# Delta rule: the meta tokens' inverse moved out of the two-by-two level sequence, lower weight halves of the next head held back in the scan, small copies and exponentials moved between engines

## The reference, cut to what matters

```python
qkv = silu(depthwise_conv(concat([q, k, v]), conv_w))     # 5 taps
q, k = l2norm(q) * DN_DK ** -0.5, l2norm(k)
b = cumsum(g)                                            # per chunk
dec = where(incl, exp(b_i - b_j), 0)
A = where(strict, (k * beta) @ k.T * dec, 0)
sol = triangular_solve(A + I, rhs)                       # the inverse
attn = (q @ k.T) * dec
def step(S, inp):                                        # over chunks
    v_new = uc - wc @ S
    o = qd @ S + attn @ v_new
    S = S * cd + kd.T @ v_new
```

## Time and profile before

| | us |
|---|---|
| median of 3 runs | 2447.34 |
| lowest and highest of them | 2438.19, 2450.72 |
| the profiled execution's own time | 2440.41 |
| its span | 2438.6 |

### The profile page before, as it was taken

The page is one execution under the profiler, slowest core; times in us unless marked ns, Lnnn a source line. Parts: engine busy times, 40 slices in busy tenths (PEclk is TensorE's granted clock), DMA queues, the critical chain, the costliest instruction groups (busy, mean ns, idle before and its releaser), DMA issues. The chain is left out here.

```text
span 2438.6 us, 43070 instructions
## 1 busy us (share of the span) xinstructions
PE 2276.5 (93%) x14129; PEld 1347.7 (55%) x14129; DVE 1612.6 (66%) x3480; ACT 1011.7 (41%) x1779; POOL 1037.3 (43%) x732
## 2 busy tenths in 40 slices
PE   7999998996888888888999999998999999999998
PEld 6444444455767777774465556555666544444443
DVE  7535333115666666661522798898999589999887
ACT  4322323314343434423313433437899544443331
POOL 4421421414444445434613687776676422222220
PEclk9999999998999999999999999999999999999999
DMA  5311311311110111004331698888999799999994
GB/s 200 120 53 51 103 55 55 104 51 34 35 35 26 34 34 34 9 1 139 121 113 45 191 316 283 283 291 266 385 395 353 241 368 383 385 388 388 344 358 151
DMA packets 174313, 440.38 MB, mean 181 GB/s; under 512 B 17408, under 2 KB 83584, under 8 KB 174096
## 3 DMA queue, kind: packets, MB, share of 16 engines
q1 hardware_dynamic: 132752, 288.20, 34.5%
q0 software_dynamic: 36864, 134.23, 15.3%
q10 hardware_dynamic: 4608, 16.78, 1.7%
HBM read 395.11 MB, written 44.04 MB: 180 GB/s over the span
## 5 line engine op out<-in xcount | busy, mean ns | idle before, releaser
L2193 POOL TENSOR_TENSOR hid_u_lo<-hid_u,hid_u_hi 128x1024 bf16<-128x1024 f32 x128 | 288.5, 2254 | 171.3 <-ACT hid_u_hi L2177 165.0
L150 PE MATMUL bank<-hT_hi,hid_u_hi 128*128 128x384 bf16 x1024 | 335.8, 328 | 17.8 <-POOL hid_u_lo L2193 9.6
L150 PE MATMUL bank<-hT_lo,hid_u_hi 128*128 128x384 bf16 x1024 | 335.8, 328 | 0.0
L150 PE MATMUL bank<-hT_hi,hid_u_lo 128*128 128x384 bf16 x1024 | 335.5, 328 | 0.0
L214 POOL TENSOR_TENSOR w_shared_lo<-w_raw,w_shared_hi 128x1024 bf16<-128x1024 f32 x72 | 155.0, 2172 | 360.4 <-ACT w_shared_hi L209 360.4
L2177 ACT ACTIVATE hid_u_hi<-hid_u 128x1024 bf16<-128x1024 f32 x128 | 134.9, 1055 | 210.6 <-PE bank L150 190.4
L150 PE MATMUL bank<-hT_hi,w_shared_hi 128*128 128x264 bf16 (+2 forms) x704 | 205.3, 300 | 8.5 <-ACT dn_conv_out L1512 4.6
L150 PE MATMUL bank<-hT_hi,w_shared_lo 128*128 128x264 bf16 (+2 forms) x704 | 205.2, 300 | 0.0
L150 PE MATMUL bank<-hT_lo,w_shared_hi 128*128 128x264 bf16 (+2 forms) x704 | 205.2, 299 | 0.0
L1644 POOL TENSOR_TENSOR dn_left_t<-dn_both_t,dn_masks 128x256 f32<-128x256 f32 x96 | 74.2, 794 | 286.7 <-DVE dn_both_t L1828 178.7
L2884 PE MATMUL bank<-w_shared_hi,ex_gated_hi 128*128 128x512 bf16 x384 | 146.6, 382 | 4.0 <-DVE ex_gated_lo L2966 4.0
(11 more groups left out here) (514 smaller groups left out, 5711.5 us busy)
## 6 DMA issues: line engine op xcount, KB each, us to landing
hid_u<-in_peer_u SPq DMA_DIRECT2D x128, 512.0 KB, 4.7
ex_v<-in_peer_v SPq DMA_DIRECT2D x128, 512.0 KB, 7.6
w_raw<-in_w_ret SPq DMA_DIRECT2D x60, 512.0 KB, 4.4
expert_hidden<-hid_gelu SPq DMA_DIRECT2D x128, 192.0 KB, 3.9
ex_gated<-expert_hidden SPq DMA_DIRECT2D x128, 192.0 KB, 5.4
w_raw<-in_w_dn SPq DMA_DIRECT2D x32, 512.0 KB, 4.0
expert_weights<-ex_grid ACTq DMA_DIRECT2D x32, 512.0 KB, 6.7
ex_weights<-expert_weights SPq DMA_DIRECT2D x64, 256.0 KB, 6.2
```

The source lines that it names most:

```text
L150: last = nc.tensor.matmul(out, left[l], right[r], start=start and i == 0, stop=stop and i == len(PASSES) - 1)
L2193: self.nc.gpsimd.tensor_tensor(self.us[1][:, m % 2, :, :], self.u32[:, m % RING, :, :], self.us[0][:, m % 2, :, :], ALU.subtract).then_inc ...
```

## The change

- The meta tokens get parts of their own (`meta_turn0`, `meta_first1`, ... `meta_second3`) on PE and DVE. `parts_of` gives `m` for those and `a`, `b` for all others. They stand behind other parts, one step late.
- `kkm` moves from bank 7 to bank 5, behind `kk`, and from the scan into the levels (`meta_keys` on PE, `meta` on DVE). `SCORES` becomes `scores` in the levels.
- The end of the scan on PE becomes `state4 values4 KEYS QUERIES update4 PROJ_Z6 PROJ_Z7`.
- `DECAYS_B` moves from behind `first3` to before `first4`, `DECAYS_M` from before to behind `turn4`; `token_k`, `token_v`, `token_m` move back too.
- ACT does `TAPS`, `GATES` and `head` (the copy of the scalars of this head) in place of DVE, `EXP_F` stands before `PROJ_Q`, `token_k` before `EXP_B`, and `SPLIT_V` behind `scan0`.
- DVE's `tail0` and `tail2` stand behind `second1` and `second3`.
- POOL waits before the three lower weight halves of the next head until `CONV_2.3` is done.

```diff
-                             ("bb", 6), ("bm", 6), ("nq", 2), ("ss", 3), ("nk", 3), ("nm", 5), ("z", 6), ("kk", 5)], DH)
-        order = [("kkm", 7), ("qk", 7), ("tk", 0), ("tv", 0), ("tm", 0)]
+                             ("bb", 6), ("bm", 6), ("nq", 2), ("ss", 3), ("nk", 3), ("nm", 5), ("z", 6), ("kk", 5), ("kkm", 5)], DH)
+        order = [("qk", 7), ("tk", 0), ("tv", 0), ("tm", 0)]
...
-        pe_levels = ("turn0 PROJ_Q.0 PROJ_Q.1 first1 PROJ_Q.2 second1 PROJ_Q.3 turn1 PROJ_Q.4 DECAYS_F first2 PROJ_Q.5 "
-                     "second2 PROJ_Q.6 PROJ_Q.7 turn2 tail PROJ_K.0 first3 PROJ_K.1 DECAYS_B second3 PROJ_K.2 PROJ_K.3 "
-                     "turn3 token_k PROJ_K.4 first4 PROJ_K.5 PROJ_K.6 second4 PROJ_K.7 DECAYS_M turn4 token_v PROJ_V.0 "
-                     "PROJ_V.1 first5 PROJ_V.2 second5 PROJ_V.3 PROJ_V.4 turn5 token_m PROJ_V.5 first6 PROJ_V.6 second6 "
-                     "PROJ_V.7").split()
+        pe_levels = ("turn0 PROJ_Q.0 first1 meta_keys PROJ_Q.1 second1 PROJ_Q.2 PROJ_Q.3 "
+                     "turn1 meta_turn0 DECAYS_F PROJ_Q.4 first2 PROJ_Q.5 second2 meta_first1 PROJ_Q.6 PROJ_Q.7 "
+                     "turn2 tail PROJ_K.0 first3 meta_second1 PROJ_K.1 PROJ_K.2 second3 meta_turn1 PROJ_K.3 "
+                     "turn3 meta_first2 PROJ_K.4 DECAYS_B first4 meta_second2 PROJ_K.5 token_k second4 meta_turn2 PROJ_K.6 "
+                     "PROJ_K.7 turn4 meta_first3 DECAYS_M PROJ_V.0 first5 meta_second3 PROJ_V.1 PROJ_V.2 second5 token_v "
+                     "PROJ_V.3 turn5 PROJ_V.4 PROJ_V.5 first6 token_m PROJ_V.6 second6 PROJ_V.7").split()
         pe_scan = ("values0 PROJ_Z0 update0 PROJ_Z1 SUMS state1 values1 PROJ_Z2 update1 PROJ_Z3 state2 SCALES values2 PROJ_Z4 "
-                   "update2 state3 PROJ_Z5 values3 update3 state4 KEYS values4 PROJ_Z6 update4 PROJ_Z7 QUERIES").split()
-        act_levels = ("tail0 gate_z silu_v split_z tail1 tail2 copy_k PROJ_Q BETAS EXP_F SPLIT_Q tail3 gate_copy EXP_B PROJ_K "
-                      "SPLIT_K token_k EXP_DECAY token_v SILU_0 SILU_1 token_m PROJ_V SPLIT_V").split()
-        act_scan = "scan0 LENGTHS scan1 scan2 scan3 scan4".split()
-        dve_levels = ("turn0 conv_v tail0 first1 second1 head TAPS GATES turn1 tail1 first2 second2 turn2 CONV_0.1 ARG_F first3 "
-                      "tail2 second3 CONV_0.2 turn3 CONV_0.3 first4 CONV_0.4 ARG_B second4 CONV_1.1 turn4 CONV_1.2 ARG_M "
-                      "first5 CONV_1.3 second5 CONV_1.4 turn5 first6 second6").split()
+                   "update2 state3 PROJ_Z5 values3 update3 state4 values4 KEYS QUERIES update4 PROJ_Z6 PROJ_Z7").split()
+        act_levels = ("tail0 head gate_z silu_v TAPS GATES split_z tail1 tail2 copy_k EXP_F PROJ_Q BETAS SPLIT_Q tail3 "
+                      "gate_copy token_k EXP_B PROJ_K SPLIT_K EXP_DECAY token_v SILU_0 SILU_1 token_m PROJ_V").split()
+        act_scan = "scan0 SPLIT_V LENGTHS scan1 scan2 scan3 scan4".split()
+        dve_levels = ("turn0 conv_v first1 scores meta second1 tail0 turn1 tail1 first2 meta_turn0 second2 "
+                      "turn2 meta_first1 CONV_0.1 first3 ARG_F meta_second1 second3 tail2 meta_turn1 "
+                      "turn3 CONV_0.2 meta_first2 first4 CONV_0.3 meta_second2 second4 CONV_0.4 meta_turn2 "
+                      "turn4 ARG_B CONV_1.1 meta_first3 first5 CONV_1.2 meta_second3 second5 CONV_1.3 turn5 ARG_M CONV_1.4 "
+                      "first6 second6").split()
         dve_scan = ("scan0 CONV_2.1 state0 scan1 CONV_2.2 state1 LENGTHS scan2 CONV_2.3 state2 scan3 UNIT_K state3 UNIT_Q "
-                    "scan4 BOTH META MATRIX SCORES").split()
+                    "scan4 BOTH MATRIX").split()
...
-        def parts_of(level):
-            return [("a", 0), ("b", 1)] + ([("m", None)] if level < 4 else [])
+        def parts_of(part):
+            return [("m", None)] if part.startswith("meta") else [("a", 0), ("b", 1)]
...
+                    elif part == "head":
+                        act.wait_ge(s["head_next"], h + 1)
+                        nc.scalar.activation(hs[:, :, :], hs_next[:, :, :], ACT.Copy)
...
                         weighted_decays(more, False)
+                        pool.wait_ge(s["next_steps"], FOLLOWING_STEPS * more + FOLLOWING_DONE["BOTH"])
                         for g in range(3):
                             weights.lo(pool, more * 4 + (4 + g), g, 0)
```

More of the change, by code:

```diff
@@ L1050 @@
 MIDDLE_TAP = 2
-FOLLOWING_DONE = {"TAPS": 0, "CONV_0": 1, "CONV_1": 4, "CONV_2": 7, "BOTH": 10, "META": 11}
-FOLLOWING_STEPS = 13
+FOLLOWING_DONE = {"CONV_0": 0, "CONV_1": 3, "CONV_2": 6, "BOTH": 9}
+FOLLOWING_STEPS = 11
 def following_done(part):
@@ L1376, in second_products, with turned @@
                         bk.fills(f"z{d}{level}", last)
[L1378 to L1381, removed]
+                def turned(part, level, h):
+                    for d, i in parts_of(part):
                         if level == 0:
@@ L1451, in this @@
                 def this(part, h):
[L1452 to L1457, removed]
+                    if part == "meta_keys":
+                        early.wait_free(pe, "kkm", h)
+                        early.fills("kkm", nc.tensor.matmul(out("kkm")[0:META, 0:META], qk[:, 1, 0:META],
+                                                            qk[:, 1, 0:META], start=True, stop=True))
+                    elif "first" in part:
+                        first_products(part, int(part[-1]), h)
+                    elif "second" in part:
+                        second_products(part, int(part[-1]), h)
+                    elif "turn" in part:
+                        turned(part, int(part[-1]), h)
                     elif part.startswith("state"):
@@ L1605, in tail @@
                         nc.scalar.activation(head_of(yT, h)[0], gz[:, :], ACT.Copy).then_inc(s["y_hi"], 1)
-                run(act, "PROJ_Q PROJ_K BETAS SPLIT_Q EXP_F EXP_B EXP_DECAY SPLIT_K SILU_0 SILU_1 PROJ_V SPLIT_V LENGTHS".split(),
+                setup.wait_tables(act)
+                run(act, ("TAPS GATES PROJ_Q PROJ_K BETAS SPLIT_Q EXP_F EXP_B EXP_DECAY SPLIT_K SILU_0 SILU_1 PROJ_V "
+                          "SPLIT_V LENGTHS").split(),
                     act_levels, act_scan, this, following, tail)
@@ L1740, in following @@
                     link = Chain(dve, s["next_steps"], following_done(part), hn, FOLLOWING_STEPS)
[L1741 to L1749, removed]
+                    if part.startswith("CONV"):
                         name, _, step = part.partition(".")
@@ L1790, in following, with rights @@
                         nc.vector.reciprocal(inv_len[:, :], inv_len[:, :]).then_inc(s["len_ready"], 1)
[L1792 to L1796, removed]
+                def rights(part, level, h):
+                    for d, i in parts_of(part):
                         name = f"x{d}{level}"
@@ L1869, in this @@
                 def this(part, h):
-                    if part.startswith("turn"):
-                        rights(int(part[-1]), h)
-                    elif part.startswith("first"):
-                        masks_in(int(part[-1]), h)
-                    elif part.startswith("second"):
-                        grow(int(part[-1]), h)
+                    if part == "meta":
+                        meta_matrices(h)
+                    elif part == "scores":
+                        bk.wait_full(dve, "qk", h)
+                        bk.reads("qk", nc.vector.tensor_tensor(scores[:, :, :], by_chunk(out("qk")[:, :]),
+                                                               dec[:, :, :], ALU.mult))
+                    elif "turn" in part:
+                        rights(part, int(part[-1]), h)
+                    elif "first" in part:
+                        masks_in(part, int(part[-1]), h)
+                    elif "second" in part:
+                        grow(part, int(part[-1]), h)
                     elif part.startswith("scan"):
@@ L1907, in _ @@
                     nc.vector.memset(zeroed, 0.0)
-                nc.vector.memset(eps[:, 0:1], DK * RMS_EPS).then_inc(s["y_lo"], 1)
+                nc.vector.memset(eps[:, 0:1], DK * RMS_EPS)
                 nc.vector.memset(eps[:, 1:2], RMS_EPS)
-                nc.vector.memset(inv_len[:, :], 1.0)
+                nc.vector.memset(inv_len[:, :], 1.0).then_inc(s["y_lo"], 1)
+                dve.wait_ge(s["y_lo"], 1)
                 setup.wait_tables(dve)
                 dve.wait_ge(s["tables_in"], 32)
-                run(dve, ("TAPS GATES CONV_0 ARG_F ARG_B ARG_M CONV_1 LENGTHS CONV_2.1 CONV_2.2 CONV_2.3 "
-                          "UNIT_K UNIT_Q BOTH META MATRIX SCORES").split(), dve_levels, dve_scan, this, following, tail)
+                run(dve, ("CONV_0 ARG_F ARG_B ARG_M CONV_1 LENGTHS CONV_2.1 CONV_2.2 CONV_2.3 "
+                          "UNIT_K UNIT_Q BOTH MATRIX").split(), dve_levels, dve_scan, this, following, tail)
 MIX_FIRST = 4
```

55 lines of the change are left out of this document (27 added, 28 removed).

## The result

The changed kernel takes 2382.47 us (median of 4 runs, 2377.89 to 2387.75) against 2445.81 us for the kernel before (4 runs beside it, 2438.19 to 2450.72). The profiled execution took 2377.9 us, its span is 2376.1, 62.5 us less than before.

What follows compares the result with a forecast made beforehand. PE, busy 60.0 us of a 68.6 us turn, was taken as the bound. Per turn 10.6 gained less 5.0 lost gives 5.6; seven turns 39, with 2.0 in the prologue total 41: 2406 us, range 2388 to 2430.

Steps and rivals of the forecast that it cites:

- Waits that go: PE's queue, per full turn: eight terms, among them QUERIES 1.32 us, update0 0.60 and the lower clock 1.7, gain 10.6 us.
- values4 without KEYS: End of PE's scan: values4 idles 0.48 us where KEYS lay, less 0.2 that update4 waited before; cost 0.28 us a turn.
- meta_first2 behind tail2: Levels: after turn3 PE waits for DVE's meta copy, which now stands behind all of tail2; cost 1.65 us a turn.
- DECAYS_M behind ARG_B: Levels: PE's DECAYS_M waits for ARG_B, which now follows DVE's turn4; cost 1.75 us a turn.
- Two taps meet POOL: DVE's conv_v and CONV_1.4 meet POOL's qd and xt pairs: 0.3 to 2.4 us a turn for PE, 1.2 taken.
- state2 behind DVE's L1864: Scan: PE's wait behind a tap slowed by POOL's halves, 5.4 us in four turns, all goes: 0.86 us a turn.
- The lower clock: One stretch per turn, 3.8 us at a granted 0.55 behind a 2.1 us wait, goes: 1.7 us gained a turn.
- The last levels: After the seven full turns: QUERIES' and the meta transpose's waits go, meta_first2's comes; net change 0.
- Rival 1: Levels: new waits bring the lower clock back; in full, with taps losing, 2438 us. Chance 0.17, shared with rival 4.
- Rival 2: Whole turn: DVE's chain takes over as the bound, costing 1 us a turn, 2413 us; included in the forecast's 0.72.
- Rival 3: Second half of scan: POOL's held halves exclude DVE, PSUM readers too; slower, 2474 us. Chance 0.05, with similar waits.
- Rival 4: SCORES stays where PE waits for it, so 1.8 of the 10.6 us stay; 2419 us. Chance 0.17, shared with rival 1.

## Why the prediction was wrong

The direction and the list of waits were right; the sum was 22 us short, and the time lies 6 us below the stated range. Two terms of the sum failed: the cost put down for taps that meet POOL (1.2 us a turn, measured 0) and the gain at state2 (0.86 us a turn, measured 1.9). By the prediction's own steps:

- **Waits that go.** All of them went. update0: 0.60 was forecast (its own rows give 3.6 / 7 + 0.16 = 0.67), state1 comes 0.5 us earlier, and putting SPLIT_V back cost 0.7. QUERIES: from the state products to turn0 it is 1.40 us less, where 1.32 - 0.28 = 1.04 was forecast, a miss of 0.4 a turn. The run with QUERIES last places it: with the old order the same stretch takes 4.36 us, so the order costs 0.37, and the rest gives 1.77 instead of 1.32. Of these 0.45 the product of the meta keys, which left the scan for the levels, is 0.14 (843.51 to 843.65 before); the rest is not assigned.
- **values4 without KEYS.** 0.31 idle, as forecast (0.28).
- **meta_first2 behind tail2, DECAYS_M behind ARG_B.** 12.1 us over 7 is 1.73, 10.8 over 7 is 1.54, and with the 0.16 of each 1.89 and 1.70; forecast 1.65 and 1.75. The first wait needs a tail, so it stands in six of the seven full turns and in the last levels; over the full turns it is 1.6 a turn. Reading two in-order queues against each other gave both places and prices. One turn of the timeline:

```profile
771.98 0.37 PE L1353 MATMUL wide<-dn_x_meta,dn_l_meta 128*128 128x16 f32 x2 [1.73 <-DVE dn_x_meta L1803]
...
780.07 0.32 PE L1292 MATMUL wide<-ident,dn_scal_next_head 128*128 128x128 f32 x1 [1.53 <-DVE dn_decay L1776]
```

- **"Two taps meet POOL", 1.2 us a turn: the term that failed in the levels.** The taps met POOL exactly as described, DVE first (start, duration), then POOL:

```profile
753.66 1.40 DVE L1750 SCALAR_TENSOR_TENSOR dn_conv_out<-dn_conv_in,dn_conv_head,dn_conv_out 128x528 f32<-128x528 f32 x1
...
786.77 1.45 DVE L1750 SCALAR_TENSOR_TENSOR dn_conv_out<-dn_conv_in,dn_conv_head,dn_conv_out 128x528 f32<-128x528 f32 x1
...
798.14 0.76 DVE L1750 SCALAR_TENSOR_TENSOR dn_conv_out<-dn_conv_in,dn_conv_head,dn_conv_out 128x528 f32<-128x528 f32 x1
```

```profile
753.22 2.97 POOL L1672 TENSOR_TENSOR dn_q_decayed<-dn_exp_b,dn_q_k 128x512 f32<-128x512 f32 x2
...
803.80 6.31 POOL L214 TENSOR_TENSOR w_shared_lo<-w_raw,w_shared_hi 128x1024 bf16<-128x1024 f32 x3 [7.89 <-DVE dn_conv_out L1750]
```

  Both won at the boundary inside POOL's pair: 1.40 and 1.45 us instead of 0.76, and POOL's pair took 2.97 instead of 2.50. PE has no wait of its own in either place; the term measured 0. I had taken the middle of a range that no row of before could narrow. With it at 0 and the two waits at their size the levels' sum is 4.4 us, and 4.1 were measured. Of the 0.3 between, 0.14 is the product of the meta keys, which now stands in the levels; the rest is not assigned.
- **"state2 behind DVE's L1864 ... per turn 0.86": the term that failed in the scan.** I counted the wait in the four turns in which it shows. In the other three PE was at the lower clock for some 7 us, slower than DVE, so the same late tap cost it nothing visible; once the clock is up, it would have waited there too. The hold alone in the kernel before bears this out: it gives 1.9 us where the clock stays up and nothing in the two scans with the longest fall. From values0 to state2 the undisturbed scan of before took 11.10 us and now takes 8.72. Of these 2.4 us about 0.5 is update0's (above); the tap's share is 1.9 in every turn, 1.0 more than the 0.86 that I put down. The tap that had 3.09 us has 0.76 (798.14), and POOL's halves start 4.9 us behind its end.
- **The lower clock.** I counted 1.7 us a turn in the levels, and these stretches all went. Those behind SUMS, which some turns of before had, I left as they were. Of four scans with one (the three above and the last, where it is short enough for the wait to show) there is one left in the profiled execution: 0.2 us a turn. That is partly luck, since three are left in the other profile of the same kernel. The range's low end took in 12 us for the clock and 6 for the taps, and nothing more for state2, which is where it broke: 1.0 us in seven turns is 7 us.
- **The last levels, put at 0.** They take 1.5 us more. The 0 took QUERIES' wait off here, but it occurs eight times, in the seven full turns and in the prologue, and was counted there. What is left is meta_first2's 1.69 less the meta transpose's 0.35.

The misses are 1.2 less 0.2 in the levels (the 0.3 just named, less the 0.1 by which the two waits are smaller) and 1.0 + 0.4 + 0.2 in the scan, 2.6 in all, which is the difference between 8.2 and 5.6. Over seven turns they make up 18 of the 22 us. The last levels take 1.5 off. The rest, 5 to 6 us, no trace ties to the change: 4.4 of it is the difference of the unchanged stages between the two profiled executions.

Rival 1 (the new waits bring the clock down) didn't happen: 14 waits of 1.5 to 1.7 us in the profiled execution, and in no levels a stretch at the lower clock behind them. Rival 2 (DVE binds) shows only where a wait was taken out: e.g. the 0.52 of 1.9 us when meta_turn1 alone moved. Rival 3 (DVE held by the halves in the second half of the scan) is refuted: beside the halves its instructions, which all read PSUM, kept their durations (v_new at 806.28 takes 0.35 us, as in the earlier trace rows). Rival 4 didn't hold: SCORES no longer stands before PE's work.

## What to carry to other kernels

A wait that shows in only some turns of a loop is not worth its average: look at what hides it in the others (here the lower clock), since a change that removes the cover or shares the cause makes it worth its full size in all. Where an order is written out by hand for several engines, walk the new queues against each other with durations of the old trace; that found both new waits to within 0.3 us. And price a transfer between two engines by what stands behind it: in the levels, taking a wait out gave between a quarter and two thirds of its length, since another queue was late next.

## What was not expected of the hardware

- When a DVE instruction with two SBUF inputs meets a run of POOL instructions, who goes first at a boundary differs. Between the three lower halves (128x1024, f32 in, bf16 out) DVE lost all ten times, three in the kernel before and seven without the hold, and took up to 4.60 us instead of 0.76. Between the two instructions of qd and of xt (128x512, f32) it won in every full turn of the changed kernel in which it met them (1.40 to 1.51 us). Why is not tested.
- Behind the 18 single-column matmuls of SUMS the granted clock falls to 0.5 in some scans (one stretch of 6.7 us had a mean of 0.50 before the change) and not in others, with the same instructions ahead of it: none to six of seven scans, by kernel and by execution (one and three of seven in the two profiles of the changed kernel). A scan with it takes 1.2 to 2.9 us longer in the changed kernel and its variants.
- These falls are not most of the spread from run to run, as far as the two profiles of the changed kernel show it. They are 5.7 us apart. The seven turns, with two falls more, give 2.4 of that, the prologue 0.6, and the last scan -1.4, since the clock fell in it only in the faster execution. 4.2 us lie behind the delta rule.
- A copy of 60 columns into the next head's scalars, 1.13 us on DVE beside POOL, takes 0.30 us on ACT in its new place. On DVE at the start of the delta rule (533.55 us) it took 0.21.
